# Feed-forward input split before its norm factor, an earlier copy in the attention heads, and a softmax row scaled on VectorE

## The reference, cut to what matters

```python
x = x + merged @ w_out[l]
x = x + conv_ffn(rmsnorm(x, ffn_norm_g[l]), w_up[l], conv_w[l], conv_b[l], w_down[l])

def conv_ffn(h, w_up, conv_w, conv_b, w_down):
    gu = h @ w_up
    gate, up = gu[..., :D_FF], gu[..., D_FF:]          # D_FF = 2816 = 22 chunks of 128
    gate = lax.conv_general_dilated(...) + conv_b      # causal, width 3, each feature by itself
    return (gelu(gate) * up) @ w_down
```

## Time and profile before

| | us |
|---|---|
| median of 3 runs | 2826.54 (2825.86 to 2827.65) |
| the profiled execution | 2825.79 |
| its span in the trace | 2823.7 |
| PE busy | 2639.9 (93%) |
| DVE, ACT, POOL busy | 1283.3 (45%), 737.3 (26%), 638.8 (23%) |
| on the chain that ended last: PE, DVE, "issue", ACT | 76%, 11%, 6%, 4% |

### The profile page before, as it was taken

One profiled execution on the slowest core, in us unless ns is written; L12 is line 12 of the kernel. 1 busy time (PEld: TensorE's weight loads), 2 busy tenths in 40 slices (PEclk: granted clock), 3 DMA queues, 4 the chain that ended last, 5 costly groups with the idle time before them and its releaser, 6 DMA issues.

```text
span 2823.7 us, 33170 instructions
## 1 busy us (share of the span) xinstructions
PE 2639.9 (93%) x12374; PEld 2131.7 (75%) x12374; DVE 1283.3 (45%) x1610; ACT 737.3 (26%) x979; POOL 638.8 (23%) x360
## 2 busy tenths in 40 slices
PE   7978888999999899999999989989999999899997
PEld 4856665777878688888888877878888887677776
DVE  5653444775123543134313565246666664522243
ACT  4133333000111222011101123146566651211120
POOL 2200110333333233333333332200000003222221
PEclk9979998999999999999999989999999999999998
DMA  4100001543112111111111111100000002000011
GB/s 149 45 27 19 30 31 47 181 167 125 46 71 82 33 52 45 52 45 49 48 64 48 52 54 38 45 23 9 7 15 7 8 9 76 30 30 30 30 41 71
DMA packets 40399, 143.27 MB, mean 51 GB/s; under 512 B 4972, under 2 KB 6252, under 8 KB 39950
## 3 DMA queue, kind: packets, MB, share of 16 engines
q1 hardware_dynamic: 35724, 124.03, 13.1%
q10 hardware_dynamic: 4610, 18.35, 1.8%
HBM read 135.81 MB, written 6.55 MB: 50 GB/s over the span
## 4 chain that ended last, share of the span: by engine, by line
PE 76%; DVE 11%; issue 6%; ACT 4%; DMA 2%; DVEq 0%; ACTq 0%; SPq 0%
PE PS L437 58%; PE PS L828 3%; PE PS L768 3%; PE PS L800 2%; PE PS L776 2%; DMA AW<-in_ada 2%; ACT E L1236 1%; PE PS L478 1%; PE PS L927 1%; PE PS L923 1%; DVE cols L1850 1%; PE PS L470 1%; DVE H L1422 1%; DVE SA L1550 1%; ACT SA L1042 1%
## 5 line engine op out<-in xcount | busy, mean ns | idle before, releaser
L437 PE MATMUL PS<-H,w_hl 128*128 128x512 f32 x6624 | 1549.6, 395 | 65.3 <-DVE H L1422 16.6
L437 PEld LDWEIGHTS PS<-H,w_hl 128*128 128x128 f32 x6624 | 1254.6, 190 | 350.9 <-issue 48.2
L412 POOL CAST w_hl<-w_raw 128x1024 fp32r<-128x1024 f32 x176 | 188.2, 1069 | 2110.9 <-PE PS L437 1697.3
L414 POOL TENSOR_TENSOR w_hl<-w_raw,w_hl 128x1024 fp32r<-128x1024 f32 x176 | 441.9, 2511 | 14.1
L437 PE MATMUL PS<-FF,w_hl 128*128 128x512 f32 x1056 | 239.8, 389 | 0.0
L437 PEld LDWEIGHTS PS<-FF,w_hl 128*128 128x128 f32 x1056 | 198.3, 188 | 41.1
L768 PE MATMUL PS<-CKV,QN 128*128 128x512 f32 (+1 forms) x576 | 146.0, 367 | 4.3 <-DVE QN L1830 4.3
L828 PE MATMUL PS<-PT,CKT 128*128 128x256 f32 x960 | 122.9, 287 | 4.1 <-DVE PT L1866 4.1
L828 PEld LDWEIGHTS PS<-PT,CKT 128*128 128x128 f32 x960 | 119.2, 194 | 8.0 <-DVE PT L1866 7.3
L1866 DVE TENSOR_TENSOR PT<-PS,PT 128x512 fp32r<-128x512 f32 (+1 forms) x192 | 103.7, 596 | 34.9 <-ACT PT L1249 34.7
L768 PEld LDWEIGHTS PS<-CKV,QN 128*128 128x128 f32 x576 | 101.2, 192 | 21.8 <-issue 4.7
(11 more groups left out here) (274 smaller groups left out, 2415.5 us busy)
## 6 DMA issues: line engine op xcount, KB each, us to landing
w_raw<-in_units SPq DMA_DIRECT2D x178, 512.0 KB, 3.5
AW<-in_ada SPq DMA_DIRECT2D x48, 512.0 KB, 3.6
X<-in_x SPq DMA_DIRECT2D x8, 512.0 KB, 7.5
XIN<-in_x ACTq DMA_DIRECT2D x8, 512.0 KB, 7.0
out<-X ACTq DMA_DIRECT2D x8, 512.0 KB, 3.0
bias_scratch<-grow ACTq DMA_DIRECT2D x4, 576.0 KB, 6.5
BR<-bias_scratch ACTq DMA_DIRECT2D x4, 512.0 KB, 3.4
CXR<-in_ctx ACTq DMA_DIRECT2D x1, 1024.0 KB, 4.8
```

The lines of the kernel that those rows point to most:

```text
L412: pool.tensor_copy(hi_part, raw).then_inc(w_hi, 1)
L414: pool.tensor_tensor(lo_part, raw, hi_part.bitcast(F32), ALU.subtract).then_inc(w_split, 1)
L437: mm = pe.matmul(PS[:, out_at + a:out_at + a + m], w(s, wp, w0 + k), src[:, o:o + m], start=(k == 0 and wp == 0 and xp == 0), stop=(k == k ...
```

## The change

Three edits.

1. *Norm2.* Because the norm's factor belongs to a token and the up projection works along features, the factor can be applied behind the matmul. The residual of out1 now also splits x * ffn_g, without the factor, into `H2` (ACT high part, DVE low part), chunk by chunk while out1 runs. PE goes from out1 into the first gate unit at once; `norm_sum` follows it, and `norm_spread` follows the first up unit. ACT copies the spread factor from PSUM to `R2`. In every chunk of the feed-forward DVE now multiplies the gate by `R2` while it evacuates pair 0 (in the place of ACT's copy), and multiplies the Gelu's result by `R2` before it multiplies by pair 1. x is reloaded in single chunks into `TMP0` and `TMP1`, each issued by ACT behind its work on the turn before. To have room, `H` and the feed-forward's region change places: from here on the split input is `H2` at `F_AT`, and `FF` and all that shared its region move to `H_AT`.
2. *Absorbed weights.* On ACT `absorbed_hi(h+1)` moves from behind `normalise` of tile 5 to ahead of `mla_exp` of tile 5; on DVE `absorbed_lo(h+1)` moves ahead of `inverse` of tile 5.
3. *First tile.* Tile 0 of every head is scaled on DVE, right behind its `inverse`, and not on ACT any more.

```diff
-    XIN = at("XIN", KC * T, F_AT)
-    FF = at("FF", 2 * KC * T, F_AT, F32R)
+    R2 = TMP1
+    H2 = at("H2", 2 * KC * T, F_AT, F32R)
+    FF = at("FF", 2 * KC * T, H_AT, F32R)
...
-        phase_norm("norm2", early=before("norm2", "square") - 1)
+        def up_unit(up, i, s, first=False):
...
+            feature_major(u0 % 2, H2, KC * T, T, KC, 0, ready=before("out1", "split"), k1=KC - 1)
+            for half in range(2):
+                pe.wait_ge(lo, before("out1", "split") + KC + half)
+                mm = feature_major(u0 % 2, H2, KC * T, T, KC, 0, n=HALF * (half + 1), a0=HALF * half, opens=False,
+                                   k0=KC - 1)
+            mm.then_inc(done[0], 1)
...
+            if n == 0:
+                up_unit(up, 0, 0, first=True)
+                norm_sum(before("norm2", "norm"), before("norm2", 2), early=before("norm2", "square") - 1)
+                up_unit(up, 0, 1)
+                norm_spread(before("norm2", "norm"), before("norm2", 3))
...
+        def load_xin(s, c):
+            act.dma_start(TMP[s], t_in["x"][bass.ds(c, 1)].rearrange("o p n -> p (o n)")).then_inc(xin_in[s], 16)
...
+            def one(i, s, half=0, size=T):
...
+                act.wait_ge(x_new, i * 2 + before("out1", "xnew") + s + half + 1)
+                act.activation(H2[:, bass.ds(i * (2 * T) + o, size)], x, ACT.Copy,
+                               scale=vec[:, bass.ds(i * 2 + (VEC["ffn_g"] + s), 1)]).then_inc(hi, 1)
+                act.activation(SQ[:, half * HALF:half * HALF + size], x, ACT.Square).then_inc(sq_ready, 1)
...
-        hi_blocks(H, T, KC)
+        act.wait_ge(done[3], before("norm2", 3) + 1)
+        act.activation(R2, pair(3), ACT.Copy).then_inc(r2_ready, 1)
...
-                act.activation(SC[:, 2:2 + T], pair(0), ACT.Copy).then_inc(gp_ready, 1)
...
                     normalise(h, t + 2)
+                    if g == 1 and not last:
+                        absorbed_hi(h + 1)
                     mla_exp(h, t + 3)
                     normalise(h, t + 3)
...
-                if g == 1 and not last:
-                    absorbed_hi(h + 1)
                 latent_hi(h, g)
             if not last:
                 mla_exp(h + 1, 0)
-                normalise(h + 1, 0)
...
+                v.tensor_tensor(x, pair(s, size, half * HALF), TMP[s][:, part], ALU.add).then_inc(x_new, 1)
...
+                v.scalar_tensor_tensor(out=H2[:, bass.ds(i * (2 * T) + KC * T + o, size)], in0=x,
+                                       scalar=vec[:, bass.ds(i * 2 + (VEC["ffn_g"] + s), 1)],
+                                       in1=H2[:, bass.ds(i * (2 * T) + o, size)].bitcast(F32),
+                                       op0=ALU.mult, op1=ALU.subtract).then_inc(lo, 1)
...
-                v.wait_ge(gp_ready, i + f0 + 1)
+                v.wait_ge(r2_ready, 1)
+                v.wait_ge(done[0], i + before(up, 0) + 1)
+                chain(v.tensor_tensor(SC[:, 2:2 + T], pair(0), R2, ALU.mult))
+                v.sem_inc(free[0], 1)
...
+                act_out = SC[:, 2 * TS:2 * TS + T]
+                chain(v.tensor_tensor(act_out, act_out, R2, ALU.mult))
                 v.wait_ge(done[1], i + before(up, 1) + 1)
-                v.tensor_tensor(SC[:, 3 * TS:3 * TS + T], SC[:, 2 * TS:2 * TS + T], pair(1), ALU.mult).then_inc(xt, 1)
+                v.tensor_tensor(act_out, act_out, pair(1), ALU.mult).then_inc(xt, 1)
...
+        def first_tiles(h, t):
+            v.wait_ge(rc_ready, h * 8 + (t + 1))
+            e = E[:, t * TK:(t + 1) * TK]
+            v.tensor_scalar(e, e, cols[:, 24 + t:25 + t], None, ALU.mult).then_inc(e_ready, 1)
...
                     peak(h, t + 3)
-                    inverse(h, t + 3)
                     if g == 1 and not last:
                         absorbed_lo(h + 1)
+                    inverse(h, t + 3)
...
                 peak(h + 1, 0)
                 inverse(h + 1, 0)
+                first_tiles(h + 1, 0)
                 gated(h, 1)
                 peak(h + 1, 1)
```

More of the change, by code:

```diff
@@ L74 @@
     ("msplit", {"split": 8}),
-    ("out1", {0: 4, 1: 5, "unit": 8, "xnew": 9, "square": 9}),
-    ("norm2", {**NORM, "split": 8}),
+    ("out1", {0: 4, 1: 5, "unit": 8, "xnew": 9, "square": 9, "split": 9}),
+    ("norm2", {**NORM}),
     ("up0", {0: 8, 1: 8, "unit": 16, "split": 8}),
@@ L661, in _ @@
         project("out1", 0, H, KC, before("out1", "split"), halves=True)
-        phase_norm("norm2", early=before("norm2", "square") - 1)
+        def up_unit(up, i, s, first=False):
+            u0 = before(up, "unit")
+            take(s, i + b(up, s))
+            pe.wait_ge(w_split, i * 2 + u0 + s + 1)
+            if not first:
+                feature_major((u0 + s) % 2, H2, KC * T, T, KC, s * 1024).then_inc(done[s], 1)
+                return
+            feature_major(u0 % 2, H2, KC * T, T, KC, 0, ready=before("out1", "split"), k1=KC - 1)
[4 more added lines that the diff above has]
+            mm.then_inc(done[0], 1)
         for n, chunks in enumerate(FF_PASSES):
             up, down = f"up{n}", f"down{n}"
-            with pe.Fori(0, chunks) as i:
-                u0 = before(up, "unit")
+            if n == 0:
[3 more added lines that the diff above has]
+                norm_spread(before("norm2", "norm"), before("norm2", 3))
+            with pe.Fori(0 if n else 1, chunks) as i:
                 for s in range(2):
[L668 to L671, removed]
+                    up_unit(up, i, s)
             project(down, 2, FF, chunks, before(down, "split"), halves=n == len(FF_PASSES) - 1)
@@ L1704, in residual, with attn_residual, one @@
                 v.sem_inc(acc_ready, 1)
-        residual("out1", 0, other=XIN)
-        phase_scale("norm2", D, 1e-6)
-        apply_split(H, KC * T, X, KC, T, lambda c: v1("ffn_g", c))
+        def attn_residual():
+            chain(v.memset(ACC, 0.0))
+            def one(i, s, half=0, size=T):
+                o, part = s * T + half * HALF, slice(half * HALF, half * HALF + size)
+                x = X[:, bass.ds(i * (2 * T) + o, size)]
+                v.wait_ge(done[s], i + before("out1", s) + half + 1)
+                v.wait_ge(xin_in[s], i * 16 + 16)
+                v.tensor_tensor(x, pair(s, size, half * HALF), TMP[s][:, part], ALU.add).then_inc(x_new, 1)
+                n = i * 2 + s + half + 1
+                v.wait_ge(x_new, n + before("out1", "xnew"))
+                v.sem_inc(free[s], 1)
+                v.wait_ge(hi, n + his[0])
+                v.scalar_tensor_tensor(out=H2[:, bass.ds(i * (2 * T) + KC * T + o, size)], in0=x,
+                                       scalar=vec[:, bass.ds(i * 2 + (VEC["ffn_g"] + s), 1)],
+                                       in1=H2[:, bass.ds(i * (2 * T) + o, size)].bitcast(F32),
+                                       op0=ALU.mult, op1=ALU.subtract).then_inc(lo, 1)
+                v.wait_ge(sq_ready, n + sqs[0])
+                v.tensor_tensor(ACC[:, part], ACC[:, part], SQ[:, part], ALU.add).then_inc(sq_added, 1)
+                v.wait_ge(sq_added, n + acs[0])
+            turns = KC // 2 - 1
+            with v.Fori(0, turns) as i:
+                for s in range(2):
+                    one(i, s)
+            one(turns, 0)
+            for half in range(2):
+                one(turns, 1, half, HALF)
+            sqs[0] += KC + 1
+            acs[0] += KC + 1
+            his[0] += KC + 1
+            v.sem_inc(acc_ready, 1)
+        attn_residual()
+        scale_diagonal("norm2", D, T)
         chain(v.memset(SC[:, 0:2], 0.0))
```

167 lines of the change are left out of this document (85 added, 82 removed).

## The result

The changed kernel takes 2811.53 us (median of 4 runs, 2805.14 to 2813.69), the kernel before 2826.25 on the same chip (2825.86 to 2827.65). The ratio is 0.9945, with a 95% interval of 0.9931 to 0.9959: 14.7 us faster, where 7.9 was forecast. The profiled execution, the slowest of the four, spans 2811.9 us, against 2823.7.

A forecast was written before the change was run, and what follows sets the result against it. PE, busy 93% of the span, bounds the kernel, so only its idle or slowed time counts. -13.3 - 9.0 - 0.5 + 8.9 + 6 = -7.9 us from 2825.79 gives 2817.9, stated as 2818.5; range 2808 to 2828.

The forecast's parts named there:

- Norm2, -13.3: Out1 to the third feed-forward unit: 14.6 us gained on PE, less 1.3 for later effects; bounds -12.1 and -14.6.
- the 1.3 put down for what comes behind it: Behind norm2's 2.8 us gap: a pair 1 stall of 0 to 1 us and a clock loss of 0 to 1.5.
- The feed-forward loop, nothing: Feed-forward chunks: DVE's two added multiplications, about 2.4 us, are covered by PE's 21.8 us; costed at nothing.
- POOL's subtraction was to end when it did: Feed-forward chunks: POOL's subtraction follows PE and ends when it did before; costed at nothing.
- Absorbed weights, -9.0: Attention heads: PE's wait for absorbed weights goes, 7 x 1.28 us; bounds 0 and -9.1.
- First tile, -0.5 + 8.9: Tile 0's scaling on DVE: first head gains 0.5; POOL collision and queued gate product cost 7 x 1.27 at head changes.
- The clock, +6: Head changes: PE's clock falls behind the longer gap before tile 0, 5 of 7 heads at 1.2 us each; bounds 0 and +10.5.
- The clock holding in the heads (2812): Rival, heads: no clock fall, 6 us less and 0.7 less in norm2, 2812; chance 16%.
- No collision (2805): Rival, head changes: DVE's tile 0 scaling not held up by POOL, -21.6 us, 2805; chance 10%.
- A fall at all seven changes: Rival, heads: every clock fall costs the full 1.5 us and norm2 has its lower bound, -2.2, 2824.5; chance 12%.
- a clock that stays low through a head: Rival, heads: PE stays at the lower level through tiles 0 and 1, losing 3.4 us per head, 2836.5; chance 7%.
- turns of out1 held up by x: Rival, out1: x loaded chunk by chunk holds turns up, 2 us over six turns, +12, 2830.5; chance 5%.

The follow-up runs named there:

- n2_only: The changed kernel with the absorbed-weights and first-tile edits undone, so the norm2 edit alone: 2813.19 us, ratio 0.9951.
- t0_only: The kernel before with the first-tile edit alone (tile 0 scaled on DVE): 2837.35 us, ratio 1.0037.
- no_t0: The changed kernel with the first-tile edit undone (tile 0 scaled on ACT again): 2801.34 us, ratio 0.9906.
- both_spread: As both, with norm2's factor spread inside the first up unit, behind 6 of its 8 chunks, not behind it: 2794.74 us, ratio 0.9892.
- both: The changed kernel with the gate product moved ahead of tile 0's reciprocal on DVE and POOL's split released by tile 3's scores: 2796.86 us, ratio 0.9899.
- ah_only: The kernel before with the absorbed-weights edit alone: 2816.36 us, ratio 0.9961.
- gate_first: The changed kernel with the last head's gate product moved ahead of tile 0's reciprocal on DVE, POOL's split left in place: 2808.13 us, ratio 0.9941.

## Why the prediction was right, and where it was off

*Norm2, -13.3.* Alone it measured -13.3, known to 4 to 5 us, so that it meets the forecast to the decimal is luck. The mechanism was right: PE runs on, and one gap is left (2.60 for 2.8). In the 1.3 put down for what comes behind it, the clock was too cheap and the stall too dear: the fall costs 1.7, more than the 1.5 named as its most, and the late release of pair 1 did not show in the changed kernel, presumably because the fall of the clock gave DVE the time. It showed once the gap was gone (0.39 us). In the traces the part is worth less than the median says: from the start of out1 to the first sums behind the feed-forward it is 828.9 us before (844.15 to 1673.09), 816.2 in `n2_only` (844.72 to 1660.95) and 817.5 in the changed kernel (844.77 to 1662.29), so 12.7 and 11.4. The 1.3 between these two is the slower start of out1: the clock was at 0.50 over its first 6 us there, and at 0.72 in `n2_only` and in the kernel before. It is not bound to part 1, since `t0_only`, without it, was at 0.50 as well; but six of the seven traced kernels with part 1 and one of the three without it started like that, so whether the part makes it more frequent stays open.

*The feed-forward loop, nothing.* It held (21.76 us a chunk, as before), and the reason given was right: DVE's new multiplication behind the Gelu fills the time in which DVE waited for PE. A chunk of the changed kernel, which answers to the earlier trace rows:

```profile
1071.14 1.15 ACT L1194 ACTIVATE SC<-SC,vec 128x1024 f32<-128x1024 f32 x1
1072.40 1.23 DVE L1799 TENSOR_TENSOR SC<-SC 128x1024 f32<-128x1024 f32 x1 [2.67 <-ACT SC L1194]
1073.75 1.22 DVE L1801 TENSOR_TENSOR SC<-SC,PS 128x1024 f32<-128x1024 f32 x1
1074.01 1.04 POOL L414 CAST w_hl<-w_raw 128x1024 fp32r<-128x1024 f32 x1 [6.79 <-PE PS L439]
```

In the kernel before, PE's finishing of pair 1 released DVE's multiplication (1084.43) and then POOL's copy, at 1084.82. If the copy comes 0.39 behind here as well (an estimate from these two times), DVE could have started at 1073.62; it had just ended its multiplication with `R2`, at 1073.63, and started at 1073.75. So the multiplication from PSUM is some 0.1 us late, with a whole unit to spare. One reading did not hold, without harm: POOL's subtraction was to end when it did, and beside DVE's new timing it takes 2.90 in one of the two units of this chunk (from 1064.32), where it took 2.40 in both.

*Absorbed weights, -9.0.* Alone it measured -10.1; 7 x 1.28 is within its interval, and so is 7 x 1.43 = 10.0, which the head periods give. The waits are gone and none came in their place.

*First tile, -0.5 + 8.9.* The mechanism was as forecast: 1.96 us for 2.0, the scaling ending 0.69 behind POOL for 0.69, a gap of 2.44 for 2.6. Two experiments separate it from the queue's order. Each head lost 1.13 in place of 1.27.

*The clock, +6.* This term was mis-sized, and by this trace it carries most of the miss of 7 us. The step was "5 of 7 heads and 1.2 each". In the changed kernel's trace the clock fell behind two of the seven gaps. Head by head, from one tile 0 to the next:

```profile
1921.86 1.67 PE L818 MATMUL PS<-ident,E 128*128 128x128 f32 x10 [2.44 <-DVE G L1954]
...
1980.76 2.40 PE L818 MATMUL PS<-ident,E 128*128 128x128 f32 x10 [2.37 <-DVE G L1954]
...
2039.75 1.31 PE L818 MATMUL PS<-ident,E 128*128 128x128 f32 x10 [2.44 <-DVE G L1954]
```

```profile
1921.80:1926.40 4.60, 4.54 (x18) 3.93 (x19) 3.99 (x8) 2.78 (x5) 0.00 (x0) 0.63 0.31 106
1980.70:1985.40 4.70, 4.64 (x19) 4.19 (x20) 3.50 (x8) 2.78 (x5) 0.00 (x0) 0.64 0.29 104
2039.70:2044.30 4.60, 4.20 (x25) 3.58 (x25) 4.24 (x8) 2.67 (x5) 0.00 (x0) 1.00 0.27 105
```

The gaps are alike to 0.1 us and what follows them is the same work; only the clock differs. The two heads behind the falls lasted 58.90 and 58.99 us, the four behind the next gaps 57.96 to 58.10: 2 x 0.9 us was paid, where 6.0 had been put down. In `t0_only`, with gaps of the same length, it was 5 x 1.0. So the forecast's count was a possible one, but not the one of this kernel's profiled execution, and the 1.2 for each was a little high. Why one gap of 2.4 us is followed by a fall and the next is not stays open, and with it how many heads are hit in a single execution. Such falls are not needed to account for the width of the changed kernel's times (8.5 us from 2805.14 to 2813.69, against 1.8 in the four runs before): `no_t0`, with gaps of 1.3 us at the changes of heads and the clock at 1.00 behind them, spread over 8.2 us, and the kernel before, in the ten executions beside it, over 7.1. `both_spread` spread over 1.6 us in its four, `both` over 6.3.

The first head shows more than 0.5: its gap before tile 0 is 1.53 where it was 2.03, and its ten transposes ran at full clock, 1.31 us, where they had taken 1.92. Only a part of that is the change's. The kernels that kept ACT's scaling had a gap of 1.72 to 1.82 there and no fall of the clock, so part 3 brought 0.2 to 0.3 and the rest lay in that one execution of the kernel before:

```profile
1863.84 1.31 PE L818 MATMUL PS<-ident,E 128*128 128x128 f32 x10 [1.53 <-DVE E L1932]
```

*The sum.* The parts alone measured -13.3, -10.1 and +10.9, together -12.5, against -14.7 for the whole and -7.9 forecast. The first difference is inside the intervals. Of the second, by the trace, 4 us are the clock term, 1 the shorter gaps, 1 or so the first head. This accounts for one execution and is set against a difference of medians: the traced execution of the changed kernel was the slowest of four, and stages with the same instructions differ by some microseconds from one execution to the next, as the last section shows. The gain was nearly twice the one forecast; that the time still lay between 2808 and 2828 is owed to the width of that range.

*The rivals.* The clock holding in the heads (2812) came nearest by its number, though the clock did fall twice. No collision (2805) is refuted by the 1.96 us. A fall at all seven changes is refuted by the five at 1.00, a clock that stays low through a head by periods of at most 58.99 us, and turns of out1 held up by x by the unbroken stream of 432 matmuls. The rule of the Trainium skill (SBUF, State Buffer, "SBUF: two separate sides") on the port pair decided the collision rightly: the earlier trace rows had shown it for one shape, and L1932 shows it for the other, together with its exception, since the gate product from PSUM took 0.69 under POOL before. The rule of the Trainium skill on the clock (TensorE: Matmul & The Clock Gate, Part 1), by which it would have held behind all seven gaps, describes five of these heads and not the other two: behind 2.4 us of idling the granted clock was 0.63 and 0.64 in those, and 1.00 in the five.

## What to carry to other kernels

Before work is moved to VectorE, look at what GpSimd runs at that moment: here a float32 scaling between SBUF tiles was done only 0.7 us behind the end of GpSimd's subtraction (1.96 us for 0.89), and a product with one operand in PSUM was not held up (0.69). The same scaling made the kernel 10.9 us slower under GpSimd's split, made no difference once the split was released two tiles later (2801.73 against the 2801.34 of `no_t0`), and brought 0.47 us a head once the gate product was out of its way as well. And a change made of several parts should be timed in parts: here one of three took back what another gave while the whole still looked like a success.

A per-token factor can go behind a matmul, which turned this norm between two projections from a stop of 21 us into 3.7 us of extra matmuls and one gap of 2.6; the gap goes too, if the spreading is put inside a unit and not at its end.

## What the runs showed that was not expected

PE's clock also fell where PE had not idled at all. In the changed kernel it was 0.51 from 1769.0 to 1772.5, behind 20 matmuls with a single column each (the sums of a norm), in a stretch in which the trace shows PE busy throughout:

```profile
1765.88 0.94 PE L472 MATMUL PS<-ones,SC 128*128 128x1 f32 x8
...
1767.13 1.03 PE L472 MATMUL PS<-ones,SC 128*128 128x1 f32 x8
```

```profile
1766.00:1769.00 3.00, 3.00 (x25) 2.85 (x24) 0.39 (x2) 2.78 (x4) 0.29 (x1) 1.00 0.00 0
1769.00:1772.50 3.50, 3.50 (x10) 2.68 (x10) 3.46 (x2) 1.02 (x1) 3.18 (x2) 0.51 0.00 0
```

That is 10 matmuls in 3.5 us, where the next 3.5 us held 17, and the unit of 48 took 12.79 us where it takes 11.19 at full clock: 1.6 us. The kernel before and `t0_only`, with the same instructions, had a clock of 1.00 there, and the other seven traced kernels a clock of 0.51 to 0.55. `ah_only` is among them, which is the kernel before up to this point, so the fall needs none of the three parts; whether it is chance that all seven kernels with part 1 have it, and that the narrow matmuls stand ahead of it, was not tested.

Larger differences lie ahead of it. Out1 starts at 844.77 in the changed kernel and at 840.81 in `gate_first`, and at 844.15 in the kernel before and 846.95 in `ah_only`, where the instructions up to there are the same in each of the two pairs. So 3 to 4 us of the difference between two executions can lie in stages that nobody touched, which is why the terms above are read from stretches of the trace and not from its ends.
